# Four more q tiles made in pairs, five weight chunks a head instead of six, and a new order of the engines over four heads

## The reference

```python
h = rmsnorm(x, pre_norm_g)
proj = h @ w_in            # q, k, v, z_attn, z_ssm: 2048 columns each, then x/B/C and dt
o = dilated_attention(q, k, v, rel_bias_table)       # 16 heads of 128
attn_out = rmsnorm(o, attn_norm_g) * silu(z_attn)
ssm_out = ssd_branch(z_ssm, xbc, dt_raw, ...)        # conv, chunked scan in both directions, gate, norm
mix = concatenate([attn_out, ssm_out]) @ w_out
return x + rmsnorm(mix, post_norm_g)
```

## Time and profile before

| | before |
|---|---|
| median of 3 runs | 2412.13 us (2411.86 to 2412.84) |
| profiled execution | 2410.25 us, span 2408.4 us |
| PE busy | 2385.9 us, 99% |
| weight loads of PE busy | 2268.8 us, 94% |
| DVE busy | 1803.3 us, 75% |
| ACT busy | 997.4 us, 41% |
| POOL busy | 472.4 us, 20% |
| granted clock of PE | 0.999 |

### The profile page before, as it was taken

The page is one execution under the profiler, slowest core; times in us unless marked ns, Lnnn a source line. Parts: engine busy times, 40 slices in busy tenths (PEclk is TensorE's granted clock), DMA queues, the critical chain, the costliest instruction groups (busy, mean ns, idle before and its releaser), DMA issues.

```text
span 2408.4 us, 36470 instructions
## 1 busy us (share of the span) xinstructions
PE 2385.9 (99%) x13604; PEld 2268.8 (94%) x13604; DVE 1803.3 (75%) x2582; ACT 997.4 (41%) x1665; POOL 472.4 (20%) x756
## 2 busy tenths in 40 slices
PE   7999999999999999999999999999999999999998
PEld 6999999999999999999999999999999988888887
DVE  5686776566666777777767888888888868787767
ACT  6323433333333333333335555555555533334332
POOL 0000177787776111111100000000000000000000
PEclk9999999999999999999999999999999999999999
DMA  5234466666666444444457566666565435445544
GB/s 165 79 105 158 142 193 205 199 206 201 204 207 197 124 122 129 122 122 122 122 167 238 168 189 199 198 197 189 172 218 171 160 127 175 158 157 130 175 166 158
DMA packets 321050, 399.61 MB, mean 166 GB/s; under 512 B 23414, under 2 KB 242870, under 8 KB 317991
## 3 DMA queue, kind: packets, MB, share of 16 engines
q1 hardware_dynamic: 266103, 225.20, 30.9%
q0 software_dynamic: 29456, 96.41, 12.9%
q10 hardware_dynamic: 25376, 76.53, 9.4%
HBM read 309.42 MB, written 95.98 MB: 168 GB/s over the span
## 4 chain that ended last, share of the span: by engine, by line
PE 98%; DVE 1%; ACT 0%; DMA 0%; SPq 0%; issue 0%; DVEq 0%
PE ps L1163 41%; PE ps L1030 17%; PE ps L1325 14%; PE ps L911 8%; PE ps L1249 5%; PE ps L1131 2%; PE ps L1050 2%; PE ps L1087 2%; PE ps L1068 1%; PE ps L1142 1%; PE ps L933 1%; PE ps L861 0%; PE ps L1058 0%; PE ps L1093 0%; PE ps L947 0%; PE ps L1358 0%
## 5 line engine op out<-in xcount | busy, mean ns | idle before, releaser
L1163 PE MATMUL ps<-h_hi,w_hi 128*128 128x384 f32 x1088 | 365.2, 336 | 0.0
L1163 PE MATMUL ps<-h_lo,w_hi 128*128 128x384 f32 x1088 | 364.9, 335 | 0.0
L1163 PE MATMUL ps<-h_hi,w_lo 128*128 128x384 f32 x1088 | 364.6, 335 | 0.0
L2439 DVE TENSOR_TENSOR w_lo<-raw_qk,w_hi 128x512 fp32r<-128x512 f32 x272 | 216.0, 795 | 143.0 <-ACT w_hi L1688 141.8
L1163 PE MATMUL ps<-t_hi,w_lo 128*128 128x384 f32 x816 | 276.0, 338 | 0.0
L1163 PE MATMUL ps<-t_hi,w_hi 128*128 128x384 f32 x816 | 275.6, 338 | 0.0
L1163 PE MATMUL ps<-t_lo,w_hi 128*128 128x384 f32 x816 | 275.0, 337 | 0.0
L1688 ACT ACTIVATE w_hi<-raw_qk 128x512 fp32r<-128x512 f32 x272 | 171.2, 630 | 243.2 <-PE ps L1163 243.2
L1163 PEld LDWEIGHTS ps<-h_lo,w_hi 128*128 128x128 f32 x1088 | 204.4, 188 | 0.0
L1163 PEld LDWEIGHTS ps<-h_hi,w_lo 128*128 128x128 f32 x1088 | 204.2, 188 | 0.0
L1163 PEld LDWEIGHTS ps<-h_hi,w_hi 128*128 128x128 f32 x1088 | 204.2, 188 | 0.0
(11 more groups left out here) (368 smaller groups left out, 5350.7 us busy)
## 6 DMA issues: line engine op xcount, KB each, us to landing
raw_qk<-in_w_in SPq DMA_DIRECT2D x102, 512.0 KB, 4.4
w_raw<-in_w_in SPq DMA_DIRECT2D x144, 256.0 KB, 7.6
stage<-loc_scr ACTq DMA_DIRECT2D x32, 768.0 KB, 7.1
stage<-t_scr SPq DMA_DIRECT2D x48, 512.0 KB, 3.8
stage<-in_w_out SPq DMA_DIRECT2D x36, 512.0 KB, 3.7
stage<-zx_scr ACTq DMA_DIRECT2D x46, 384.0 KB, 8.8
stage<-in_w_in SPq DMA_DIRECT2D x34, 512.0 KB, 4.2
zx_scr<-w_raw SPq DMA_DIRECT2D x34, 384.0 KB, 3.4
```

Source lines behind the costliest of these rows:

```text
L1163: ins = nc.tensor.matmul(ps[:, bank, 0:HALF_T], w, h(k), start=(start and kk == 0 and q == 0), stop=(last and kk == KC - 1 and q == 2), sk ...
L2439: nc.vector.tensor_tensor(w_lo[:, n_slot(n, pp), :], src, w_hi[:, n_slot(n, pp), :].bitcast(f32), ALU.subtract).then_inc(w_lo_done, 1)
```

## The change

q of the heads 2, 6, 10 and 14 is made in two more pairs (kind `"qe"`). The stream keeps q of heads 4, 8 and 12 only, 16 chunks fewer in all, so each head has 5 chunks. A tile is 4 chunks, so the place in a head at which a tile begins and ends now repeats every four heads, and the order of roundings on ACT and DVE is written by `a % 4`. PE has 3, 2, 1 and 2 halves at its places in a head where it had 4, 2, 1 and 3, and the turns of x and v have a half between them. On ACT, `stream_hi(m)` comes ahead of the exponentials, the sample's probabilities are normalised by ACT, and `squared` moves from ahead of the transposes of x to behind all loads. On DVE, `biased_maxima` comes ahead of `y_gated_by`, `square_added` moves behind v, and `attention_gated` from ahead of `across_read` to the end.

```diff
+Q_MADE = [_i for _i in range(HEADS) if _i == 0 or _i % 4]
...
-    STREAM += [("k", _i)] if _i % 2 else [("q", _i), ("k", _i)]
+    STREAM += [("k", _i)] if _i in Q_MADE else [("q", _i), ("k", _i)]
...
-IT_CHUNKS = 6
+IT_CHUNKS = 5
...
+QE_PAIRS = 2
...
-Z_P = QQ_P + QQ_PAIRS
+QE_P = QQ_P + QQ_PAIRS
+Z_P = QE_P + QE_PAIRS
...
-                if a % 2 == 0:
+                if a + 1 in Q_MADE:
                     pool.wait_ge(pts_ready, a + 1)
                     load_q(a + 1)
...
                 scores(a)
                 scores_of_sample(a)
-                stream_halves(a, 2, 4)
+                stream_halves(a, 2, 3)
                 turn_probs(a)
-                stream_halves(a, 6, 2)
+                stream_halves(a, 5, 2)
                 turn_probs_of_sample(a)
                 attend(a)
-                stream_halves(a, 8, 1)
                 turn_x(a)
+                stream_halves(a, 7, 1)
                 if a < LAST:
                     turn_v(a + 1)
-                stream_halves(a, 9, 3)
+                stream_halves(a, 8, 2)
                 across_chunks(a)
...
+            def normalised_sample(a):
+                act.wait_ge(inverted, a + 1)
+                act.wait_ge(normed, 6 * a + 4)
+                for t in range(2):
+                    nc.scalar.activation(probs_s[:, t * DEC_SEQ:(t + 1) * DEC_SEQ],
+                                         probs_s[:, t * DEC_SEQ:(t + 1) * DEC_SEQ], ACT.Copy,
+                                         scale=rinv[:, 4 + t:5 + t]).then_inc(normed, 1)
...
+                stream_hi(m)
                 exp_of_scores(a)
-                stream_hi(m)
+                exp_of_sample(a)
                 stream_hi(m + 1)
-                exp_of_sample(a)
+                normalised_sample(a)
                 probs_rounded(a)
                 exp_of_decays(a)
                 load_behind_scores(a)
                 sample_rounded(a)
-                if i % 2:
+                if a % 4 == 1:
                     k_rounded(i)
+                attended(a)
                 stream_hi(m + 2)
-                attended(a)
                 attended_sample(a)
-                squared(a)
-                stream_hi(m + 3)
                 x_turned(a)
                 v_rounded(i)
+                if a % 4 == 2:
+                    k_rounded(i)
+                load_decays(i, 1)
+                if a % 4 == 1:
+                    q_rounded(i)
                 if a > 0:
                     load_xs(i)
                 if i < LAST:
                     load_v(i + 1)
-                if i % 2 == 0:
+                squared(a)
+                if a % 4 in (0, 2, 3):
                     q_rounded(i)
+                stream_hi(m + 3)
+                stream_hi(m + 4)
+                if a % 4 in (0, 3):
+                    k_rounded(i)
                 silu_of_gates(a)
-                load_decays(i, 1)
-                stream_hi(m + 4)
-                stream_hi(m + 5)
...
                     y_summed(a - 1)
+                biased_maxima(a)
+                if a > 0:
                     y_gated_by(a - 1)
-                biased_maxima(a)
                 biased_maxima_of_sample(a)
                 decay_differences(a, 1)
+                sums_inverted(a)
                 normalised(a)
-                stream_lo(m)
+                sums_of_sample_inverted(a)
                 decay_differences(a, 0)
                 decay_limited()
-                normalised_sample(a)
                 probs_lo(a)
-                stream_lo(m + 1)
...
+                stream_lo(m)
+                stream_lo(m + 1)
                 sample_lo(a)
                 weighted_decays(a)
-                if a < LAST:
-                    square_added(a)
...
                 v_lo_of(i)
-                if i % 2 == 0:
+                if a % 4 == 3:
+                    q_lo_of(i)
+                square_added(a)
+                if a % 4 == 1:
+                    k_lo_of(i)
+                if a % 4 == 2:
                     q_lo_of(i)
                 stream_lo(m + 2)
+                if a % 4 == 0:
+                    q_lo_of(i)
                 stream_lo(m + 3)
-                if i % 2:
+                stream_lo(m + 4)
+                across_read(a)
+                if a % 4 in (0, 2, 3):
                     k_lo_of(i)
-                stream_lo(m + 4)
+                if a % 4 == 1:
+                    q_lo_of(i)
+                skip_added(a)
                 attention_gated(a)
-                across_read(a)
```

More of the change, by code:

```diff
@@ L86 @@
            tuple((ZX_Q + 1 + 2 * n - 4 * QQ_P) * P for n in range(2))),
+    "qe": (8 * P, tuple(COL_Q + (2 + 4 * n - 8 * QE_P) * P for n in range(2)),
+           tuple((ZX_Q + 2 + 4 * n - 8 * QE_P) * P for n in range(2))),
     "z": (P, (COL_ZA - Z_P * P, COL_ZS - Z_P * P), ((ZX_ZA - Z_P) * P, (ZX_ZS - Z_P) * P)),
@@ L462, in encoder @@
         LAST = HEADS - 1
-        q_loads = lambda i: 1 + (i + 1) // 2
+        q_loads = lambda i: sum(q <= i for q in Q_MADE)
+        q_first = lambda i: i == 0 or i % 4 in (0, 1)
         bank_of = lambda pp, b: 3 * pp + b
@@ L724, in _ @@
             pair_transfers(QQ_P, "xs", "qq", "qq")
-            with sp.Fori(QQ_P + 1, Z_P - 1) as p:
+            with sp.Fori(QQ_P + 1, QE_P - 1) as p:
                 pair_transfers(p, "qq", "qq", "qq")
-            pair_transfers(Z_P - 1, "qq", "qq", "z")
-            pair_transfers(Z_P, "qq", "z", "z")
+            pair_transfers(QE_P - 1, "qq", "qq", "qe")
+            pair_transfers(QE_P, "qq", "qe", "qe")
+            pair_transfers(Z_P - 1, "qe", "qe", "z")
+            pair_transfers(Z_P, "qe", "z", "z")
             with sp.Fori(Z_P + 1, NP - 1) as p:
@@ L1042, in scores @@
                 pe.wait_ge(tile_out, tile_of("k", a) + 1)
[L1043 removed]
+                if a in Q_MADE:
                     pe.wait_ge(q0_out, q_loads(a))
@@ L1607, in q_rounded @@
             def q_rounded(i):
-                if i == 0 or i % 2:
+                if i in Q_MADE:
                     act.wait_ge(q0_in, 16 * q_loads(i))
@@ L1868, in _ @@
             load_head(LAST)
+            stream_hi(STREAM_CHUNKS - 1)
             exp_of_scores(LAST)
-            stream_hi(STREAM_CHUNKS - 2)
-            stream_hi(STREAM_CHUNKS - 1)
             exp_of_sample(LAST)
+            normalised_sample(LAST)
             probs_rounded(LAST)
@@ L2310, in biased_maxima_of_sample, with sums_inverted, normalised @@
                 nc.vector.tensor_scalar(nmx[:, 4:6], mx[:, 4:6], -1.0, None, ALU.mult).then_inc(negmax, 1)
-            def normalised(a):
+            def sums_inverted(a):
                 dve.wait_ge(probs_exp, 6 * a + 4)
                 did(nc.vector.reciprocal(rinv[:, 0:4], lsum[:, 0:4]))
+            def normalised(a):
                 settle()
@@ L2318, in normalised, with sums_of_sample_inverted @@
                                             rinv[:, t:t + 1], None, ALU.mult).then_inc(normed, 1)
-            def normalised_sample(a):
+            def sums_of_sample_inverted(a):
                 dve.wait_ge(probs_exp, 6 * a + 6)
[L2322 to L2327, removed]
+                nc.vector.reciprocal(rinv[:, 4:6], lsum[:, 4:6]).then_inc(inverted, 1)
             def probs_lo(a):
@@ L2342, in q_lo_of @@
             def q_lo_of(i):
-                if i == 0 or i % 2:
-                    dve.wait_ge(qk_hi_done, 2 * i + 2 if i else 1)
+                if i in Q_MADE:
+                    dve.wait_ge(qk_hi_done, 2 * i + (1 if q_first(i) else 2))
                     nc.vector.scalar_tensor_tensor(q_lo[:, :], raw_qk[:, T:2 * T], Q_SCALE, q_hi[:, :].bitcast(f32),
@@ L2347, in q_lo_of @@
                 else:
-                    tile_lo(2 * i, parity_of("q", i), q_lo, q_hi, Q_SCALE)
+                    tile_lo(2 * i + (0 if q_first(i) else 1), parity_of("q", i), q_lo, q_hi, Q_SCALE)
             def k_lo_of(i):
-                tile_lo(2 * i if i % 2 else 2 * i + 1, parity_of("k", i), k_lo, k_hi, 1.0)
+                tile_lo(2 * i + (1 if q_first(i) else 0), parity_of("k", i), k_lo, k_hi, 1.0)
             def v_lo_of(i):
```

12 lines of the change are left out of this document (1 added, 11 removed).

## The result

The changed kernel takes 2419.38 us in the median (2416.99 to 2423.5) against 2412.07 us for the kernel before (2410.24 to 2413.11) on the same chip: ratio 1.0032, 95% interval 1.0023 to 1.0042. I had forecast 2411.3 us, no change that can be measured, and a range up to 2418. The time lies outside the range, and on the side to which I had given 0.19.

The account below looks back on a forecast made before the run. TensorE, holding 98% of the chain, was taken as the bound. Its own time gave -7.4 us and stalls of scores behind the late square +6.6, so -0.8 us in all: 2411.3 us, range 2404.5 to 2418.

Parts of the forecast that it names:

- the side to which I had given 0.19: Whole kernel: slower than the kernel before by over 0.2%, through rival B or rival C; chance 0.19.
- PE's own time: TensorE alone: heads 4.14 us shorter (-66.2 over 16), two more pairs +58.8, so -7.4 us.
- Softmax, ACT's normalisation, DVE up to v: Each head ahead of across_chunks: all hidden, turn_probs by 0.5 us; v_lo ends 25.85 us after scores starts.
- The square: ScalarE: six DMA issues hold it until 26.32 us after scores starts; scores then stalls 0.37 us a head.
- rival B: ScalarE's sixth issue, a 768 KB broadcast, costs 0.9 us instead of 0.41; stalls 12.5 us, 2417.2 us; chance 0.14.
- The signal to PE: From the end of y_summed on VectorE to the next scores on TensorE: 0.05 us, bounds 0 to 0.1.
- Heads 3, 7, 11: q_lo ahead of the square and q_hi behind squared: VectorE resumes 0.72 us later, stall 1.1 us a head.
- Head 0: First head: no load_xs ahead of the square, 0.42 us less, so no stall.
- rival C: ScalarE, heads 1, 5 and 9: q load landing after 10 us delays squared; 6.6 us more, 2417.9 us; chance 0.05.
- Rival A: ScalarE: issuing does not hold the square, so no head stalls; 2404.7 us; chance 0.27.
- The rule weighed: ScalarE's issues: by the skill's 50 ns each, six cost 0.3 us, giving 2404.7 us; set aside for the trace.

Follow-up runs that it names:

- b2: The changed kernel with the edits of e1, e3 and e4 together; 2404.55 us, 0.9968 of the kernel before.
- p2: b2 with VectorE normalising the sample, y gated ahead of the maxima and load_decays at the head's end, attention's gate left late; 2403.38 us, 0.9965 of the kernel before.
- u1: b2 with the sample's two softmax normalisations moved back from ScalarE to VectorE; 2404.6 us, 0.9965 of the kernel before.
- e1: The changed kernel with ScalarE's square moved ahead of the transposes of v and all six DMA issues; 2409.17 us, 0.9984 of the kernel before.
- e2: The changed kernel with only load_decays(i, 1) moved right behind the square; 2413.88 us, 1.0002 of the kernel before.
- t1: b2 with the square behind three DMA issues (two strips, load_decays) instead of none; 2404.73 us, 0.9969 of the kernel before.
- d1: The changed kernel with each v load split in two of half the width, eight issues ahead of the square; 2441.23 us, 1.012 of the kernel before.
- e4: The changed kernel with VectorE's sum of squares ahead of q_lo in heads 3, 7 and 11; 2418.93 us, 1.0024 of the kernel before.
- e3: The changed kernel with head 1's v loads issued at the start of head 0, not behind its softmax; 2417.94 us, 1.002 of the kernel before.

## Why the prediction was wrong, point by point

Two steps failed: the time that the six issues hold the square (3.15 us in the sum, 3.39 to 3.76 measured), and head 0, which the sum left without a stall and which lost 4.3 us. Neither alone would have taken the time out of the range.

- **PE's own time: right.** Pairs 29.38 us each, heads 36.13, and the part behind the last `scores` shorter by 3.7 us (4.1 forecast), so about -7.4 us without stalls; b2 and p2 have it (-7.7 and -8.4 by the ratios, each within some 3 us).
- **Softmax, ACT's normalisation, DVE up to v: right.** v_lo ended at 1550.20, S+25.88 against 25.85, and PE waited nowhere ahead of `across_chunks` but in head 0. u1 showed that the normalisation could as well have stayed.
- **The square: the first of two steps that failed, in its size.** The mechanism is as written, and e1, e2, t1 and d1 leave no other. But I took 3.15 us from the first strip issue to the square: 2.74 for the five issues of the earlier trace rows and 0.41 for the sixth. Measured were 3.39 to 3.76: in head 5 it is 3.44, and with the slow first matmul of the head the square starts at S+26.67 instead of S+26.32. The sixth issue itself was nearly right, 0.35 to 0.44 in its row. What I had not reckoned with is that the last issue got longer behind it: the second half load had a median of 453 ns before and 619 ns after, 0.68 in head 5. In e2, without the sixth, the same five issues took 2.74 to 3.05. The result has 0.35 of rival B's 0.49 us, but not its cause, for B had the broadcast itself at 0.9. Why the last of more issues takes longer stays open.
- **The signal to PE: 0.14 us instead of 0.05.** So a head stalls for 0.37 + 0.35 + 0.09 = 0.81 us, and 0.81 to 1.06 was measured. In a difference of two sums of 36 us, two errors of 0.35 and 0.09 doubled the result.
- **Heads 3, 7, 11: right in kind**, 1.5 us instead of 1.1 for the same reasons; e4 shows the 0.7 that q_lo's place costs.
- **Head 0: the second step that failed, a term put at nothing.** The forecast has "no stall" there, and 4.3 us were measured. I costed the loads of a head in the middle and said of head 0 only that it has an issue less. Its v load is issued in the head itself, not a head ahead, landed 10.5 us later, and was due at a turn of v that now comes at S+22.3 and not S+24.4. In the kernel before it landed 8.6 us after its issue at 1291.78, 0.15 us ahead of the turn. By e3 it is 4.0 us, of which some 1.7 were the clock.
- **The q load (rival C): hidden.** The twelve loads from head 0 on landed after 7.2 to 8.4 us where the nine of before had 6.1 to 7.7; why, no run shows. That of head 5 was issued at 1541.11 and landed 7.8 us later, at 1548.9. The row of `q_hi` names it, but the issue of `load_decays` ahead of `q_hi` held ACT until 1549.22, and `q_hi` started at 1549.27: the load cost nothing.
- **Rival A** did not come. The rule weighed against the trace was answered by d1: two issues more, 20 us more in the heads, at the same bytes. The section of the Trainium skill's "DMA: Bandwidth & Descriptors", "Anatomy of one DMA", from which I took the 50 ns, describes DMAs issued by GpSimd, and these are issued by ScalarE: it was no price for them. The Trainium skill, "Perfetto Trace Analysis", section "DMA Instruction — HWDGE (DVE, Sync)", says that the issuing sequencer is free for the next instruction only at the end of the profiled window of a DMA; the trace agrees, since the square starts 0.09 us behind the last issue (1550.22 + 0.68, then 1550.99).
- **The gate's move:** in my text it is only part of a reordering, and it is worth 7 to 10 us. I costed each moved instruction for what it adds, not for what it would have cost where it was.

## What to carry to other kernels

A few DMA issues ahead of an instruction that another engine waits for can hold it for 0.33 to 0.75 us each (the rows of after; up to 1.24 in d1): write them behind it, and make few of them. The Trainium skill, "Perfetto Trace Analysis", section "DMA Optimizations", says that splitting DMAs may let the whole finish sooner where the DMA engines are generally idle; on a queue that shares its engine with work on the path, d1 lost 22 us by it. An issue that goes out while its engine still has work costs nothing in these traces: in the kernel before, `load_decays` is written behind the silu of the gates, was issued at 1505.73 while `q_hi` ran, and silu started at 1507.75. When a stage gets shorter, go through every wait in it that ended just in time, in the first head too, and ask for each instruction which other engine's result it needs and what stands behind it: here the exchange of chunks for pairs brings its 7.4 us only if the square is early, the gate late and head 0's load early. Where a forecast is a small difference of long sums, its error is that of the sums: 0.35 us in heads of 36 and one load forgotten turned "no change" into slower.

## What the runs showed of the hardware

- In the medians an issue takes ACT a time that hardly depends on its bytes: half loads (of 384 columns) had medians of 454 and 619 ns, quarter loads (192 columns, d1) 506 and 567 ns (rows of their source lines from 1370 us on, the two tiles apart). The same instruction differs by more than that: the longest quarter load took 1235 ns.
- TensorE fell to its lower clock after a single wait of 2.40 us inside a stretch in which it had been fully busy (granted clock 0.56 in the 3.3 us from 1360.70). The same fall stands in e1, e2, e4 and d1, whose wait for this load is 2.5, 2.2, 2.2 and 3.0 us long, and in none of the runs that have the load early. In head 1 of d1 TensorE stood for 1.64 us ahead of `within_chunks`, and the clock stayed at 1.00:

```profile
1410.20:1411.87 1.67, 0.03 (x2) 0.00 (x1) 1.67 (x4) 1.02 (x2) 0.00 (x0) 1.00 0.55 161
1411.87:1413.40 1.53, 1.53 (x25) 1.36 (x25) 1.53 (x3) 0.00 (x0) 0.00 (x0) 1.00 0.98 296
```

So a wait can cost more than its length, and the waits of 0.6 to 1.0 us of the other heads did not.
